# Both attentions of the first layer in one loop: a unit of each kind per step, weighted values with tokens on the partitions, head norm per query tile, half of the modulation's sums on GpSimd

## The reference

```python
# A, differential attention: two score matrices of depth 32 for each head, over all 768 keys
s = einsum('bqhcd,bkhcd->bhcqk', q, k) * (32 ** -0.5)
p = softmax(s, axis=-1)
a = p[:, :, 0] - lam * p[:, :, 1]
o = einsum('bhqk,bkhd->bqhd', a, v)
o = rmsnorm(o, subln_g) * (1.0 - lam_init)        # over the 64 values of a head
# B, neighbourhood attention: one score matrix of depth 64, a bias on the 512 keys that aren't context
s = concat(q @ k_ctx * scale, q @ k_win * scale + bias)   # -inf outside the window
o = softmax(s) @ v
# modulation: six vectors of 1024 that scale, shift and gate; the last four are needed from w_out on
mod_l = split(silu(c) @ ada_w + ada_b, 6)
x = x + g1 * (concat([a, b, pool, hyena]) @ w_out)
```

## Time and profile before

| | us |
|---|---|
| median of 3 runs (2760.93 to 2763.34) | 2761.19 |
| the profiled execution, its own time | 2758.17 |
| span of its instructions | 2756.0 |
| PE busy / DVE / ACT / POOL | 2551.9 / 966.8 / 527.0 / 65.1 |

### The profile page before, as it was taken

How to read it: one execution, slowest core, us unless ns; L and a number is a source line. 1 busy time by engine, 2 the same in 40 slices (tenths; PEclk the granted TensorE clock), 3 DMA queues, 4 the chain that set the end, 5 groups by cost and what they waited for, 6 DMA issues and landing times.

```text
span 2756.0 us, 31092 instructions
## 1 busy us (share of the span) xinstructions
PE 2551.9 (93%) x11540; PEld 1924.5 (70%) x11540; DVE 966.8 (35%) x1743; ACT 527.0 (19%) x1095; POOL 65.1 (2%) x163
## 2 busy tenths in 40 slices
PE   7999977787999996977989999989999989899999
PEld 3565455546888884864778888847657668788888
DVE  7231277522000003126253443333323443534432
ACT  2200043321112113154121110012122110221100
POOL 1000000000111110000000000000000000000000
PEclk9999978896999997987999999999999999999999
DMA  9202123105999894210222222221211202222221
GB/s 328 99 8 62 54 72 90 54 0 193 331 329 333 327 329 179 69 31 1 62 69 77 91 79 75 91 100 54 82 48 53 76 24 105 79 92 85 84 82 63
DMA packets 83346, 307.12 MB, mean 111 GB/s; under 512 B 9264, under 2 KB 9264, under 8 KB 82624
## 3 DMA queue, kind: packets, MB, share of 16 engines
q1 hardware_dynamic: 75888, 274.24, 29.7%
q0 software_dynamic: 7376, 31.77, 2.9%
HBM read 292.86 MB, written 13.11 MB: 111 GB/s over the span
## 4 chain that ended last, share of the span: by engine, by line
PE 87%; DVE 7%; ACT 3%; issue 2%; DMA 1%; SPq 0%; DVEq 0%; POOL 0%; ACTq 0%; POOLq 0%
PE products L1197 37%; PE products L788 12%; PE products L1078 9%; PE products L942 7%; PE products L1090 4%; PE products L989 2%; PE products L961 2%; PE products L1323 2%; PE products L1267 1%; PE products L852 1%; PE products L896 1%; PE products L906 1%; PE products L803 1%; PE products L1181 1%; PE products L1311 1%
## 5 line engine op out<-in xcount | busy, mean ns | idle before, releaser
L1197 PE MATMUL products<-normed,ring 128*128 128x264 f32 (+1 forms) x1312 | 303.9, 388 | 11.3 <-DVE normed L2289 11.3
L1197 PEld LDWEIGHTS products<-normed,ring 128*128 128x128 f32 x1312 | 252.1, 193 | 56.1 <-issue 16.0
L1419 ACT ACTIVATE arena<-products 128x264 f32<-128x264 f32 (+3 forms) x263 | 118.6, 468 | 729.8 <-PE products L788 203.0
L1078 PEld LDWEIGHTS products<-arena,ring 128*128 128x128 f32 x2176 | 248.3, 194 | 8.8 <-issue 8.8
L1078 PE MATMUL products<-arena,ring 128*128 128x128 f32 x2176 | 248.6, 277 | 0.8 <-ACT arena L1534 0.8
L788 PE MATMUL products<-normed,ring 128*128 128x264 f32 (+2 forms) x736 | 219.7, 462 | 3.5 <-DVE normed L1726 3.5
L788 PEld LDWEIGHTS products<-normed,ring 128*128 128x128 f32 x736 | 141.6, 193 | 81.5 <-issue 65.6
L942 PE MATMUL products<-ring,normed 128*128 128x512 f32 (+1 forms) x416 | 182.5, 599 | 8.4 <-DVE normed L1726 8.4
L1197 PE MATMUL products<-arena,mixed 128*128 128x256 f32 (+1 forms) x832 | 189.4, 382 | 0.0
L1197 PEld LDWEIGHTS products<-arena,mixed 128*128 128x128 f32 x832 | 158.1, 190 | 23.8
L1197 PE MATMUL products<-normed,mixed 128*128 128x264 f32 (+1 forms) x704 | 161.5, 383 | 0.0
(11 more groups left out here) (424 smaller groups left out, 2827.9 us busy)
## 6 DMA issues: line engine op xcount, KB each, us to landing
ring<-in_weights SPq DMA_DIRECT2D x303, 512.0 KB, 4.1
ring<-in_experts SPq DMA_DIRECT2D x204, 512.0 KB, 5.0
arena<-results SPq DMA_DIRECT2D x8, 512.0 KB, 7.6
residual<-in_x POOLq DMA_DIRECT2D x1, 2048.0 KB, 16.2
arena<-in_dft_half POOLq DMA_DIRECT2D x1, 2048.0 KB, 8.4
token_rows<-arena SPq DMA_DIRECT2D x4, 512.0 KB, 2.9
out<-residual SPq DMA_DIRECT2D x8, 256.0 KB, 4.6
arena<-in_bias POOLq DMA_DIRECT2D x1, 1920.0 KB, 24.5
```

Of the source, the lines that this page charges most:

```text
L1078: m = pe.matmul(ps[:, side, m_ * P:(m_ + 1) * P], w[:, k, :], job_t[:, k, :], start=(k == 0), stop=(k == KT - 1))
L1197: m = pe.matmul(bank(p, n), left(k), right(k), start=(fresh and k == 0), stop=(k == kt - 1), skip_group_check=True)
L1419: act.activation(out, src, ACT.Copy, scale=scale).then_inc(bank_free[p.bank], 1)
```

## The change

**Steps.** `UNITS` gives way to `STEPS`, 16 pairs (query tile, head) with all heads of a tile together; a step does one A unit and one B unit. A's scores take three banks (0 to 2) and B's two (3 and 4), the transposes of both kinds banks 5 and 6, the weighted values of both bank 7. The order of A's four score matmuls is interleaved between its two halves; as both halves write bank 1, one of them waits for another (`half_scored`).

**Scaling.** The row's reciprocal is no longer applied to the probabilities. For A one operation with three inputs joins the two matrices (the second times `-lam * sum0 / sum1`); for B DVE does nothing to them, and PE transposes the exponentials as they are. ACT applies the reciprocal when it copies the weighted values out of PSUM.

**Token-major.** The weighted values' operands change places: weights are now the 128 x 128 transposed probabilities, the moving operand the 64 columns of values, and the result has tokens on the partitions (`o_tok`). The norm by head is taken on it for each query tile: DVE squares and sums (128 x 256), ACT does `Ln` and `Exp` on 128 x 4 numbers, DVE scales, PE transposes the tile's A and B halves back to feature-major, ACT copies them to `mix`. Three of the four tiles do so inside the loop, behind step 5, 9 and 13.

**Modulation.** Of the 32 tiles DVE does the even ones, one for each step, and GpSimd the odd ones, with a multiplication into `mod_term` and an addition into `acc2` for each. The order of the tiles in the stream changes so that two running sums are made side by side.

**Set-up.** DVE's set-up moves ahead of its reads of the pooling products.

The diff, cut to its core:

```diff
@@ plan() @@
+    def scores(s, kind):
+        if s < len(STEPS):
+            r["scores", s, kind] = b.take(0, 1, 2) if kind == "A" else b.take(3, 4)
+    def turned(s, kind):
+        r["T", s, kind] = [b.take(5), b.take(6)]
+    def weighed(s, kind):
+        if s >= 0:
+            r["PV", s, kind] = b.take(7)
...
+STEPS = [(t, h) for t in range(ST) for h in range(HEADS)]
+OUT_AT = {HEADS * t + 5: t for t in range(ST - 1)}
+def mod2_tile(j):
+    return 2 * (j % 2) + j // 16, j // 2 % 8
@@ gpsimd @@
+            pool.wait_ge(silu_ready, 1)
+            ready(pool, r["scores", 0, "A"])
+            for j in range(1, 32, 2):
+                n = START["mod2"] + j
+                part, k = mod2_tile(j)
+                w = ring[:, n % RING, :]
+                pool.wait_ge(landed[n % RING], 16 * (n // RING + 1))
+                if k == 0:
+                    pool.tensor_scalar(acc2[:, part], w, silu_c[:, k, 0:1], None, ALU.mult).then_inc(mod_added, 1)
+                else:
+                    pool.tensor_scalar(mod_term, w, silu_c[:, k, 0:1], None, ALU.mult).then_inc(mod_scaled, 1)
+                    pool.wait_ge(mod_scaled, j // 2 - part + 2)
+                    pool.tensor_tensor(acc2[:, part], acc2[:, part], mod_term, ALU.add).then_inc(mod_added, 1)
+                pool.wait_ge(mod_added, j // 2 + 1)
@@ tensor, attentions() @@
+                        m = pe.matmul(ps[:, p.bank, 0:DH], prob_t[:, a, kt, :], vals[:, kt, a, h * DH:(h + 1) * DH],
+                                      start=(kt == 0), stop=(kt == NKT - 1))
...
+                def feature_major(t):
+                    pe.wait_ge(sub_done, t + 1)
+                    read(pe, r["PV", HEADS * t + 3, "B"])
+                    for a, p in enumerate(r["OT", t]):
+                        fill(p)
+                        for c in range(2):
+                            m = pe.transpose(ps[:, p.bank, c * P:(c + 1) * P], o_tok[:, t % 2, a, c * P:(c + 1) * P], ident)
+                        finish(p, m)
...
+                for s in range(len(STEPS)):
+                    scores(s + 1, "A")
+                    turn(s, "A")
+                    if s > 0:
+                        weigh(s - 1, "B")
+                    scores(s + 1, "B")
+                    turn(s, "B")
+                    weigh(s, "A")
+                    if s in OUT_AT:
+                        feature_major(OUT_AT[s])
+                weigh(len(STEPS) - 1, "B")
                 p = r["mod2"]
+                fill(p)
+                pe.wait_ge(mod_read, 16 + 16)
+                pe.wait_ge(mod_added, 16)
                 for i in range(32):
...
-                for c, p in enumerate(r["subln"]):
-                    fill(p)
-                    pe.wait_ge(sub_sq, 1)
-                    finish(p, pe.matmul(bank(p), head_ones, prob_sq[:, c], start=True, stop=True))
+                feature_major(ST - 1)
@@ scalar, attentions() @@
+                for s in range(len(STEPS)):
+                    turned(s, "A")
+                    if s > 0:
+                        weighed(s - 1, "B")
+                    exps(s + 1, "A")
+                    turned(s, "B")
+                    exps(s + 1, "B")
+                    weighed(s, "A")
+                    if s % HEADS == 0 and s > 0:
+                        roots(s // HEADS - 1)
+                    if s in OUT_AT:
+                        feature_major(OUT_AT[s])
+                weighed(len(STEPS) - 1, "B")
+                roots(ST - 1)
+                feature_major(ST - 1)
@@ vector, attentions() @@
+                def joined(s):
+                    read(dve, r["scores", s, "A"])
+                    sums, inv = row_sum[:, s % 2], row_inv[:, s % 2]
+                    link(dve.reciprocal(inv[:, 0:2], sums[:, 0:2]))
+                    link(stt(inv[:, 1:2], inv[:, 1:2], neg_lam, sums[:, 0:1], ALU.mult, ALU.mult))
+                    stt(prob_a[:, 0], prob_a[:, 1], inv[:, 1:2], prob_a[:, 0], ALU.mult, ALU.add).then_inc(prob_ready, 1)
...
+                for s in range(len(STEPS)):
+                    joined(s)
+                    if s in OUT_AT:
+                        head_norm(OUT_AT[s])
+                    maxima(s + 1, "A")
+                    if s % HEADS == 0 and s > 0:
+                        head_squares(s // HEADS - 1)
+                    mod2_term(2 * s)
+                    read(dve, r["scores", s, "B"])
+                    dve.reciprocal(row_inv[:, s % 2, 2:3], row_sum[:, s % 2, 2:3]).then_inc(inv_b, 1)
+                    maxima(s + 1, "B")
+                head_squares(ST - 1)
+                head_norm(ST - 1)
```

More of the change, by code:

```diff
@@ new lines, in turn @@
+                def turn(s, kind):
+                    of = prob_a[:, 0] if kind == "A" else prob_b
+                    if kind == "A":
+                        pe.wait_ge(prob_ready, s + 1)
+                    else:
+                        read(pe, r["scores", s, "B"])
+                    for j, p in enumerate(r["T", s, kind]):
+                        fill(p)
+                        for kt in range(4 * j, min(4 * j + 4, NKT)):
+                            m = pe.transpose(ps[:, p.bank, (kt % 4) * P:(kt % 4 + 1) * P], of[:, kt * P:(kt + 1) * P], ident)
+                        finish(p, m)
@@ L967, in attentions @@
+                scores(0, "A")
                 read(pe, r["bq"][1])
@@ L1492, in attentions @@
                 act.activation(lam_t[:, 66:68], lam_t[:, 64:66], ACT.Exp).then_inc(lam_exp, 1)
-                unit = [0]
-                def exps(i):
-                    for c, p in enumerate(r["scores", i]):
-                        unit[0] += 1
-                        act.wait_ge(max_ready, unit[0])
-                        act.activation(prob[:, i % 2, c], wide(p, NKEY), ACT.Exp, bias=neg_max[:, i % 2, c:c + 1],
-                                       accum_out=row_sum[:, i % 2, c:c + 1]).then_inc(bank_free[p.bank], 1)
@@ L1512, in attentions, with exps @@
-                root(r["subln"], [(0, S), (S, S)], sub_rs_t)
+                def exps(s, kind):
+                    if s == len(STEPS):
+                        return
+                    p = r["scores", s, kind]
+                    act.wait_ge(max_a if kind == "A" else max_b, s + 1)
+                    for c in range(2 if kind == "A" else 1):
+                        i = c if kind == "A" else 2
+                        to, of = (prob_a[:, c], wide(p, 2 * NKEY)[:, c * NKEY:(c + 1) * NKEY]) if kind == "A" else (prob_b, wide(p, NKEY))
+                        ins = act.activation(to, of, ACT.Exp, bias=neg_max[:, s % 2, i:i + 1], accum_out=row_sum[:, s % 2, i:i + 1])
+                    ins.then_inc(bank_free[p.bank], 1)
@@ new lines, in turned, with weighed @@
+                def turned(s, kind):
+                    for j, p in enumerate(r["T", s, kind]):
+                        n = 4 if j == 0 else 2
+                        copy(p, prob_t[:, "AB".index(kind), 4 * j:4 * j + n], bank(p, n * P).rearrange("p (k q) -> p k q", k=n))
+                def weighed(s, kind):
+                    t, h = STEPS[s]
+                    if kind == "B":
+                        act.wait_ge(inv_b, s + 1)
+                    p = r["PV", s, kind]
+                    copy(p, o_tok[:, t % 2, "AB".index(kind), h * DH:(h + 1) * DH], bank(p, DH),
+                         row_inv[:, s % 2, 0:1] if kind == "A" else row_inv[:, s % 2, 2:3])
@@ new lines, in roots, with feature_major @@
+                def roots(t):
+                    act.wait_ge(sub_sum, t + 1)
+                    act.activation(sub_ln, sub_ms, ACT.Ln, bias=eps, scale=1.0 / DH).then_inc(sub_logs, 1)
+                    act.wait_ge(sub_logs, t + 1)
+                    act.activation(sub_rs, sub_ln, ACT.Exp, scale=-0.5).then_inc(sub_root, 1)
+                def feature_major(t):
+                    for a, p in enumerate(r["OT", t]):
+                        copy(p, mix[:, 2 * a:2 * a + 2, t * P:(t + 1) * P], bank(p, 2 * P).rearrange("p (c q) -> p c q", c=2),
+                             sub_g if a == 0 else 1.0)
@@ L1737, in mod_terms @@
                     dve.wait_ge(landed[n % RING], 16 * (n // RING + 1))
[L1738 to L1740 removed]
+                    for v in range(2):
+                        acc = acc1[:, part, v]
+                        last_v = v == 1
                         if k == 0:
```

247 lines of the change are left out of this document (117 added, 130 removed).

## The result

The changed kernel takes 2787.47 us (median of 4, 2786.33 to 2791.72) beside 2762.27 us of the kernel before on the same chip (median of 4, 2760.93 to 2769.14): a ratio of 1.010, 95% interval 1.0082 to 1.0118. It is slower by 25 us where 64 us less was forecast, and outside the range of 2686 to 2726.

A forecast was written before the change was run, and what follows sets the result against it. PE fills first: sixteen steps of 7.56 us (121.0), turning back 1.5, start 2.5 and 0.7, roots 6.3, GpSimd 2.4, clock 2.0: loop 136.4. With an end of 11.0, `w_out` comes 64.0 us earlier: 2697 us, range 2686 to 2726.

The forecast's parts named there:

- the clock's: Loop: PE at half clock for 4 us around the first and longest pause of 2.5 us, costing 2.0 us.
- Rival 3: Loop: clock goes to and fro as in A's units, mean 0.77; PE step 9.8, 30 us more, 2727; chance 0.08.
- The root, GpSimd and clock terms: Loop: roots 6.3 us over three times, DVE late beside GpSimd 2.4, half clock 2.0, added to PE's steps.
- Set-up: Start of the stage: DVE's set-up moves into time without DVE work; first maximum at about 340.4 instead of 345.40.
- PE's step: Loop: scores 1.50, transposes 0.78, weighted values 1.50 for each of two kinds; 7.56 us a step.
- DVE and ACT: Loop: DVE needs 6.4 us and ACT 5.3 us a step, both less than PE's 7.56.
- Roots and turning back: Three times in the loop: roots cost 6.3 us together (bounds 2 and 9), the transposes turning tiles back 1.5.
- rival 2: Loop: DVE and GpSimd hinder each other, DVE's join and tile double, DVE 8.7 us a step; 2720; chance 0.13.
- the sign by which it was to be known: Loop: DVE's 768-column join taking longer than 1.02 us would show DVE and GpSimd hindering each other.
- Rival 1: Loop: ACT's function switches cost twice 1.31 us; six switches make 7.9 us more, 2705; chance 0.09.
- Rival 4: Modulation: GpSimd too slow; a tile over 8.4 us decides the end, above 12.4 no gain; chance 0.04.
- The end: Loop's end to `w_out`: modulation's sum 9.26 us, then last transposes and copies 1.7; 11.0 together, `w_out` at 486.0.

The follow-up runs named there:

- the last kernel: Changed kernel, token-major weighted values kept, but 128 columns of values moving instead of 64 (the head's and its neighbour's): 2703.71 us, ratio 0.9797 to the kernel before.

## Why the prediction was wrong

**The step that failed** is the clock's: "Now the longest pause is the first, 2.5 us; I take 4 us of PE at half clock there, 2.0." The pause came (2.37 us ahead of 344.10) and so did the fall, at 342.0, but the clock did not rise again while token-major products of 64 columns filled the loop, though PE had nothing but work. Rival 3 named the place and was set aside with "a PE that is the bound doesn't pause": true of the pauses (0.4 us in all from 344.1 to 564.9), but pauses are not all that decides. The 4 us had no row behind them either: before, the clock stayed at 0.50 for 13.7 us behind the first pause, and in the last kernel of the experiments, where it does come back, it is low for the same 13.7 us. An estimate from that kernel's rows: its first full step lasts 11.6 us for records that take 6.2 at full clock, and the next 8.2 instead of 7.6, so the first fall costs some 6 us there and not 2.0. The likeness was wrong too, "these are much the same instructions": the weighted values are 24 of a step's 48 records of PE, and their operands had changed places. Its price, 2727 at a mean of 0.77, was too mild as well: the clock went to 0.50 and did not come and go.

A hint stood in the rows of the kernel before. The forecast priced the new weighted values by the modulation's sum, 64 records with 128 x 128 weights and one moving column, and saw that its later part ran at half clock. PE was busy from 531.8 to 541 there without a pause, and the clock fell at 536.6 in the midst of it; in the last kernel it falls at 488.0, likewise amid that sum and with PE busy. So records that load full weights for few moving columns had gone together with a falling clock before, on a PE that was the bound. The forecast took the cost from this row and not the question.

**Its price.** The loop was to end at 475.0; the modulation's sum starts at 564.89, 89.9 later. Sixteen steps of 14.0 instead of 7.56 are 103.0. The root, GpSimd and clock terms (6.3 + 2.4 + 2.0 = 10.7) are swallowed by a slower PE and go off. The first scores of both kinds still ran at full clock (3.3 instead of 6.15, 2.8 less), and the start's pauses were 0.8 shorter than 3.2. Turning back cost 3 x 0.85 = 2.6 instead of 1.5. 103.0 - 10.7 - 2.8 - 0.8 + 1.1 = 89.8. That it meets 89.9 so closely is luck: the stage began 0.3 us earlier than taken and PE waited 0.4 us near its end, which nearly cancel and are not in the sum. Behind it the sum took 13.55 instead of 9.26, as it now ran at half clock from its first record, 4.3 more. Together 94.2, and this execution's own 2788.41 less the forecast's 2694.2 is 94.2.

**Set-up**: right. First maximum at 340.29 (forecast 340.4), and alone it gave 0.28%.

**PE's step**: right in sum at full clock (7.4 with 64 columns, 7.6 with 128, against 7.56), by luck, as errors cancel. A's scores in their new order take 1.82 and not 1.50; weighted values and transposes are each a little shorter.

**DVE and ACT**: right in the main. Maximum 1755 ns (1.76), join 1020 (1.02), ACT's 64-column copy 314 ns (0.26). In the changed kernel neither holds PE up inside the loop, but beside a PE at half clock that says little. In the last kernel PE waits for DVE's join three times, 0.3, 0.6 and 1.0 us, and in a step of 7.6 us DVE is busy for 6.0 to 6.6 (forecast 6.4) and ACT for 4.7 to 5.0 (5.3).

**Roots and turning back**: in the last kernel, where PE is at full clock, the steps with a turning back last 10.6, 9.7 and 9.3 us against 7.6, and carry 6.9 us together (forecast 6.3 + 1.5). What the forecast lacked is what follows them: PE pauses 1.5 to 1.8 us in front of two of the three, the clock falls to 0.50 for 6.8 us each time, and the next steps last 3.2 and 4.3 us longer. The second fall, at 433.4, lies in a further pause of 1.7 us, behind which stands a late DVE (see rival 2). In front of the third PE pauses 1.1 us and the clock stays. The first of the two, with the fall at 395.8:

```profile
391.76 1.50 PE L1029 MATMUL products<-arena 128*128 128x128 f32 x12
395.01 0.63 PE L1039 MATMUL products<-const_sb,arena 128*128 128x128 f32 x4 [1.75 <-ACT arena L1488]
395.56 3.16 PE L997 MATMUL products<-arena 32*128 32x512 f32 x8
```

**Rival 1** (double switches) fell: the load takes 1283 ns and the next function follows at once (loads at 412.04 and 413.65, functions at 413.34 and 414.94).

**Rival 2** fell as a bound of every step, but its mechanism is there, and the sign by which it was to be known was blind. With GpSimd idle DVE's modulation tile takes 1277 ns; beside it, up to 3.37 us, so the 0.2 us taken for such an operation was too little. In the last kernel one such tile stands in the chain that ended last, ahead of the pause of 1.7 us in which the clock fell a second time. The join stayed at 1020 ns, but it never began amid an addition of GpSimd's in these traces: where one ran, the row scalar right ahead of the join had done the waiting (see the last section). The tile, in the last kernel:

```profile
428.00 2.34 POOL L731 TENSOR_TENSOR normed<-normed 128x1024 f32<-128x1024 f32 x1
428.05 3.37 DVE L1868 SCALAR_TENSOR_TENSOR normed<-ring,tiny,normed 128x1024 f32<-128x1024 f32 x1
...
434.83 1.51 PE L1018 MATMUL products<-const_sb,arena 128*128 128x128 f32 x6 [1.72 <-ACT mixed L1488]
```

**Rival 4** fell: GpSimd takes 5.5 us a tile and was done at 486.8 us, 78 ahead of the sum.

**The end**: 15.3 us against 11.0, all of it clock. In the last kernel, 482.59 to 492.86 is 10.3.

So the rest of the plan was sound in the main: with the clock restored it runs in 2703.7 us, 7 above the forecast, with the loop longer than forecast (336.28 to 482.42, 146.1 us against 136.4) by the falls of the clock at the start and behind the roots that are priced above.

## What to carry to other kernels

Before exchanging matmul operands, look at how many columns move for each load of weights, and read PEclk beside PE busy: a PE busy 100% at 0.50 made 390 records in the 113 us from 347 on, one busy 79% at 0.80 had made 444. When few columns move for a full load, widening the moving operand with a neighbour's columns may cost nearly nothing (0.06 us for twelve) and bring the clock back; here those two lines were worth some 84 us against the changed kernel. A pause of PE costs more than itself if the clock falls behind it (1.75 us here, and 3.2 in the next step), so a late input should be placed where PE has other work ahead of it. And when the mean of a group is the sign for contention, look at what stands right ahead of that group: another operation may take the wait.

## What the runs showed of the hardware that was not expected

- A PE that did not pause from 344.1 to 561.7 us was held at half clock all that time. Why it is held by this form of work is not settled here; shown is that the exchange of operands alone does it, and that more moving columns for the same weights undo it. The step with one dense matmul of 128 x 512 ran at either clock within one execution.
- GpSimd's multiplication of 128 x 1024 by a number for each partition took 2.84 us where nothing hindered it and 3.18 in the mean, longer than its addition of two such operands, 2.36 in the mean.
- GpSimd and DVE keep each other waiting. The means with GpSimd idle, and in the kernel with the operands swapped back while GpSimd worked (groups by shape, mean ns of one), look as if some of DVE's operations stretched and others didn't:

```profile
L1854 DVE SCALAR_TENSOR_TENSOR normed<-ring,tiny,normed 128x1024 f32<-128x1024 f32 x28 | 34.6, 1277 | 0.0
...
L2021 DVE SCALAR_TENSOR_TENSOR arena<-arena,tiny 128x768 f32<-128x768 f32 x15 | 15.3, 1019 | 0.5
...
L2020 DVE SCALAR_TENSOR_TENSOR tiny<-tiny 128x1 f32<-128x1 f32 x15 | 3.3, 220 | 0.5
```

```profile
L1868 DVE SCALAR_TENSOR_TENSOR normed<-ring,tiny,normed 128x1024 f32<-128x1024 f32 x6 | 11.0, 1840 | 0.0
L2035 DVE SCALAR_TENSOR_TENSOR arena<-arena,tiny 128x768 f32<-128x768 f32 x7 | 7.1, 1019 | 0.2
...
L2034 DVE SCALAR_TENSOR_TENSOR tiny<-tiny 128x1 f32<-128x1 f32 x7 | 4.2, 597 | 0.3
```

The modulation tile goes from 1277 to 1840 and the row scalar from 220 to 597, while the join with its two inputs stays at 1019. The single rows tell more. In the last kernel, one row scalar and the join behind it:

```profile
368.09 2.36 POOL L731 TENSOR_TENSOR normed<-normed 128x1024 f32<-128x1024 f32 x1
369.17 1.30 DVE L2034 SCALAR_TENSOR_TENSOR tiny<-tiny 128x1 f32<-128x1 f32 x1
370.50 1.03 DVE L2035 SCALAR_TENSOR_TENSOR arena<-arena,tiny 128x768 f32<-128x768 f32 x1
370.54 3.62 POOL L729 TENSOR_SCALAR normed<-ring,tiny 128x1024 f32<-128x1024 f32 x1
```

The row scalar, 0.22 us by itself, begins amid GpSimd's addition and ends at 370.47, 0.02 us behind the addition's end. Every row scalar that began amid an addition, in this trace and in that of the kernel with the operands swapped back, ends 0.01 to 0.03 us behind it, and a modulation tile that does ends 1.1 us behind the addition (431.42, after 430.34). Row scalars that began in the first microsecond of a multiplication end 1.12 us after its start (377.83, after 376.70, in the last kernel), and operations that began later in it are not stretched. The join follows the row scalar at once, when the wait is over, and comes through unharmed; then it is GpSimd's multiplication that takes 3.62 us instead of 2.84. Which resource the two share is not tested.
